# First expert's weights split ahead, and its first three chunks computed with the token rows stationary

## The reference

```python
x = x + hybrid_mixer(rms_norm(x, norm_mix), ...)      # ends in concatenate([...]) @ w_out
h = rms_norm(x, norm_ffn)
affinity = softmax(h @ w_router)                      # 16 experts
g, idx = top_k(affinity.T, cap)                       # cap: 128 rows of the sample, 64 of the prompt, per expert
xe = h[idx]
he = silu(xe @ w_gate) * (xe @ w_up)                  # 1024 -> 2048
ye = (he @ w_down) * g                                # 2048 -> 1024
x = x + zeros.at[idx].add(ye)                         # then a last rms_norm
```

## Time and profile before

| | us |
|---|---|
| median of 3 runs | 2579.83 (2577.54 to 2579.99) |
| profiled execution, its own time | 2577.25 |
| its span | 2575.5 |
| TensorE busy in the span | 2520.0 (98%) |
| VectorE busy | 1649.2 (64%) |
| ScalarE busy | 1366.9 (53%) |
| GpSimd busy | 266.7 (10%) |

### The profile page before, as it was taken

The page is one execution under the profiler, slowest core; times in us unless marked ns, Lnnn a source line. Parts: engine busy times, 40 slices in busy tenths (PEclk is TensorE's granted clock), DMA queues, the critical chain, the costliest instruction groups (busy, mean ns, idle before and its releaser), DMA issues.

```text
span 2575.5 us, 45337 instructions
## 1 busy us (share of the span) xinstructions
PE 2520.0 (98%) x18610; PEld 2278.5 (88%) x18610; DVE 1649.2 (64%) x1927; ACT 1366.9 (53%) x1559; POOL 266.7 (10%) x238
## 2 busy tenths in 40 slices
PE   8999999999987999999999999999999999999998
PEld 6777777787876999999999999999999999999997
DVE  6555555435387666767666676666767666676667
ACT  6434353424445555555556555555555556555556
POOL 3102020101101010010101101010010101101010
PEclk9999999999997999999999999999999999999999
DMA  4101010135327676676767667676676767667677
GB/s 158 31 17 55 2 55 2 61 122 209 138 96 298 229 253 234 247 252 228 252 228 252 240 241 252 228 252 233 247 252 228 252 228 252 240 241 252 228 253 282
DMA packets 62486, 503.73 MB, mean 196 GB/s; under 512 B 7568, under 2 KB 8080, under 8 KB 37808
## 3 DMA queue, kind: packets, MB, share of 16 engines
q1 hardware_dynamic: 46224, 448.88, 48.0%
q0 software_dynamic: 16160, 53.38, 7.0%
HBM read 465.07 MB, written 37.22 MB: 195 GB/s over the span
## 4 chain that ended last, share of the span: by engine, by line
PE 67%; DVE 1%; ACT 1%; DMA 0%; issue 0%; POOL 0%; POOLq 0%; DVEq 0%; ACTq 0%
PE up_banks_b L2025 15%; PE up_banks_a L2025 15%; PE up_banks_b L2028 6%; PE up_banks_a L2028 6%; PE up_banks_b L2061 2%; PE up_banks_b L2060 2%; PE up_banks_b L2059 2%; PE up_banks_b L2058 2%; PE up_banks_a L2062 2%; PE up_banks_b L2062 2%; PE up_banks_a L2059 2%; PE up_banks_a L2061 2%; PE up_banks_a L2058 2%; PE up_banks_a L2060 2%; PE up_banks_b L2023 1%; PE up_banks_a L2023 1%
## 5 line engine op out<-in xcount | busy, mean ns | idle before, releaser
L1842 DVE TENSOR_TENSOR big_lo<-ew_raw,big_hi 128x4096 fp32r<-128x4096 f32 x192 | 849.6, 4425 | 419.0 <-ACT big_hi L1653 418.9
L1653 ACT CAST big_hi<-ew_raw 128x4096 fp32r<-128x4096 f32 x192 | 697.3, 3632 | 506.5 <-PE up_banks_a L2025 223.7
L2025 PE MATMUL up_banks_b<-x_parts,big_hi 128*128 128x384 f32 x2048 | 582.9, 356 | 0.0
L2025 PE MATMUL up_banks_a<-x_parts,big_hi 128*128 128x384 f32 x2016 | 573.8, 356 | 0.0
L2028 PE MATMUL up_banks_b<-x_parts,big_lo 128*128 128x192 f32 x1792 | 449.0, 251 | 0.0
L2028 PE MATMUL up_banks_a<-x_parts,big_lo 128*128 128x192 f32 x1764 | 442.0, 251 | 0.0
L2025 PEld LDWEIGHTS up_banks_b<-x_parts,big_hi 128*128 128x128 f32 x2048 | 371.0, 189 | 0.0
L2025 PEld LDWEIGHTS up_banks_a<-x_parts,big_hi 128*128 128x128 f32 x2016 | 365.1, 189 | 0.6
L2028 PEld LDWEIGHTS up_banks_b<-x_parts,big_lo 128*128 128x128 f32 x1792 | 341.4, 191 | 0.0
L2028 PEld LDWEIGHTS up_banks_a<-x_parts,big_lo 128*128 128x128 f32 x1764 | 336.1, 191 | 0.6
L64 PE MATMUL bank<-big_hi,w_hi 128*128 128x512 f32 x576 | 236.8, 411 | 0.0
(11 more groups left out here) (320 smaller groups left out, 4076.3 us busy)
## 6 DMA issues: line engine op xcount, KB each, us to landing
ew_raw<-in_expert_weights SPq DMA_DIRECT2D x192, 2048.0 KB, 7.8
w_raw<-in_w_heads SPq DMA_DIRECT2D x48, 256.0 KB, 2.8
x_in<-in_x SPq DMA_DIRECT2D x12, 512.0 KB, 4.4
x_d<-in_x POOLq DMA_DIRECT2D x12, 512.0 KB, 4.1
residual<-x_d POOLq DMA_DIRECT2D x12, 512.0 KB, 2.9
ffn_in<-h_and_xT_d POOLq DMA_DIRECT2D x12, 512.0 KB, 2.9
ew_raw<-residual SPq DMA_DIRECT2D x12, 512.0 KB, 6.7
tab<-in_tables POOLq DMA_DIRECT2D x10, 512.0 KB, 7.6
```

Of the source, the lines that this page charges most:

```text
L1653: nc.scalar.copy(w_hi[:, c % RING], raw[:, c % RAW]).then_inc(hi_done, 1)
L1842: nc.vector.tensor_tensor(w_lo[:, c % RING], raw[:, c % RAW], w_hi[:, c % RING].bitcast(F32), ALU.subtract).then_inc(lo_done, 1)
L2025: last = nc.tensor.matmul(out[:, 0:2 * CAP], hi, x[:, k], start=n == 0, stop=n == KT - 1, skip_group_check=True)
```

## The change

A new class `ExpertStart` holds what both phases now share: the routing lists, the chunk buffers and the semaphores. Chunk c of an expert now lies in block (c + 1) mod 3 of `big_hi` and `big_lo`, so that chunks 0 and 1 take the places of the sample's tokens, whose products end first. The raw chunks 0 and 1 are loaded into the very bytes where their low parts will stand (`early_raw` is the memory of `big_lo`). What moves where:

- SyncE loads chunk 0 after tile 3's product, chunk 1 after tile 7's, chunk 2 after tile 11's; chunks 3 and 4 after the sample's and the prompt's rows are gathered.
- ScalarE casts chunk 0 at the start of its tiles 5 and 6, chunk 1 at 9 and 10, four casts of two row blocks each. VectorE subtracts the first half of chunk 0 in tile 6 and the second half in tile 7; chunk 1 whole, in the experts phase.
- The token list of the sample is turned at the end of the output phase, and GpSimd's queue gathers its rows there, ahead of the last store of h. The wait for all stores goes from the end of the phase to where the prompt's rows are asked for and to ScalarE's first cast of x.
- For chunks 0 to 2 of expert 0 the token rows are stationary and the weights move: per chunk 24 matmuls of 512 columns for the sample (`sample_high` 16, `sample_low` 8) and 16 for the prompt (`prompt_both`). The results stand by tokens; SiLU and product are made there, and 12 transposes (`turn_h`) bring them to the form that the down product needs. The body of expert 0 begins at chunk 3 and is written out on all engines.
- Rows are stored sample first; the last expert's store indices are swapped to match.

```diff
+class ExpertStart:
+    def place(self, big, c):
+        first = (c + 1) % self.RING * BLK
+        return big[:, :, first:first + BLK]
+    def load_early(self, sp, c):
+        sp.dma_start(self.place(self.early_raw, c), self.weights[0, c]).then_inc(self.raw_loaded[c], 16)
...
+        WEIGHTS_HIGH = {5: (0, slice(0, 4), False), 6: (0, slice(4, KT), True), 9: (1, slice(0, 4), False), 10: (1, slice(4, KT), True)}
+        WEIGHTS_LOW = {6: slice(0, 4), 7: slice(4, KT)}
...
+                for c in range(ahead.EARLY):
+                    sp.wait_ge(filled, 2 * CH * (c + 1))
+                    ahead.load_early(sp, c)
+                sp.wait_ge(filled, 2 * TT)
+                sp.dma_start(ahead.raw[:, 2], ahead.weights[0, 2]).then_inc(ahead.raw_loaded[2], 16)
...
+                        if t == TT:
+                            pool.wait_ge(h_stored, 16 * (TT - 1))
+                            pool.wait_ge(ahead.tokens_ready, 1)
+                            pool.indirect_dma_start(ahead.xs, None, h_dram[0:SEQS[1][1]],
+                                                    bass.IndirectOffsetOnAxis(token_of[:, 0, 0:1], 0))\
+                                .then_inc(ahead.gathered, 16)
...
                     dve.wait_ge(sum_inv, t + 1)
 
+                    if t in WEIGHTS_LOW and t == S_TILES - 1:
+                        ahead.low_early(dve, 0, WEIGHTS_LOW[t]).then_inc(ahead.lo_done, 1)
                     first, _, row = LISTS[list_of(t)]
                     nc.vector.tensor_scalar(affinity[:, t - first, row:row + NE], ex[:], stat[:, RSUM, t:t + 1], None, ALU.mult).then_inc(soft, 1)
...
+        X_SAMPLE_AFTER = 3
...
                 for slot in range(1, P_SLOTS):
                     take_best(choose, nc, table, table, best, where, 2, slot, P_SLOTS)
+                    if slot == X_SAMPLE_AFTER:
+                        first_x_low(0, S_HI, H_S_LO)
...
+                dve.wait_ge(first_rows_asked, 1)
+                sample_product(0)
+                ahead.low_early(dve, 1, slice(0, KT)).then_inc(lo_done, 1)
+                first_x_low(S_FIRST, P_HI, H_P_LO)
+                split(0, 2)
+                sample_product(1)
+                prompt_sum(0)
+                split(0, 3)
...
+                            if f == 0:
+                                pe.wait_ge(p_summed, 1)
+                            else:
+                                pe.wait_ge(h_lo_done, f)
...
+                pe.wait_ge(hi_done, ahead.EARLY)
                 pe.wait_ge(turned_lo, S_FIRST)
+                sample_high(0)
+                sample_low(0)
+                sample_high(1)
+                pe.wait_ge(chosen, 2)
+                for i, lists in enumerate((chosen_gate, chosen_token)):
+                    nc.tensor.transpose(s_bank[0][:, i * ROWS:(i + 1) * ROWS], lists, ident[0:ROWS, 0:ROWS]).then_inc(back, 1)
+                pe.wait_ge(hi_done, BY_TOKENS)
+                sample_high(2)
                 pe.wait_ge(gathered, 32)
                 for r in range(KT // 2):
                     turn_prompt(r, r).then_inc(turned, 1)
+                pe.wait_ge(lo_done, 2 + RAW)
+                sample_low(1)
+                pe.wait_ge(tokens_ready, 7)
+                pe.wait_ge(turned_lo, 2 * S_FIRST)
+                prompt_both(0)
+                prompt_both(1)
+                pe.wait_ge(lo_done, BY_TOKENS + RAW)
+                sample_low(2)
+                prompt_both(2)
```

More of the change, by code:

```diff
@@ L1159, in _ @@
                     head_high(LATE_HEADS.get(t, ()))
+                    if t in WEIGHTS_HIGH:
+                        c, tiles, last = WEIGHTS_HIGH[t]
+                        for k in range(tiles.start, tiles.stop, 2):
+                            made = ahead.high_early(act, c, slice(k, k + 2))
+                        if last:
+                            made.then_inc(ahead.hi_done, 1)
                     act.wait_ge(added, 2 * t + 2)
@@ L1255, in sample_rounds @@
                             merge_lists(then, nc, best, where, 0, CAP_S, merged, spare)
+                            dve.sem_inc(ahead.chosen, 1)
                 for t in range(TT):
@@ L1277, in _ @@
                         prompt_sums((2, 3))
+                    if t in WEIGHTS_LOW and t < S_TILES - 1:
+                        ahead.low_early(dve, 0, WEIGHTS_LOW[t])
+                    if t == TT - 1:
+                        dve.wait_ge(ahead.back, 1)
+                        nc.vector.tensor_copy(token_of[:, 0:NE, 0], banks[0][:, 0:NE]).then_inc(ahead.tokens_ready, 1)
                     sample_rounds(PAUSES[t][1])
@@ L1439, in _, with experts_phase @@
                     route(t)
+                pe.wait_ge(ahead.chosen, 1)
+                pe.wait_ge(added, 2 * (TT - 2) + 1)
+                nc.tensor.transpose(banks[0][:, 0:NE], chosen_rows, ident[0:NE, 0:NE]).then_inc(ahead.back, 1)
                 turn_affinities(len(LISTS) - 1)
-def experts_phase(nc, weights, identity, norm_final, h_dram, acc, outs, routing, big_hi, big_lo):
+def experts_phase(nc, weights, norm_final, h_dram, acc, stored, outs, ahead):
     with ExitStack() as ctx:
@@ L1493, in experts_phase @@
         const_loaded = sem("const_loaded_f")
[L1494 to L1496 removed]
+        raw_loaded, hi_done, lo_done = ahead.raw_loaded, ahead.hi_done, ahead.lo_done
         chunk_done = sem("chunk_done")
@@ L1644, in body @@
                     pool.sem_inc(rows_free, 1)
-                experts(pool, body)
+                experts(pool, body, first=0)
             @block.scalar
@@ L1732, in end_squares, with first_x_high @@
                     end_prompt_square(i)
-                split(0, 0)
-                for first, cols in ((0, S_HI), (S_FIRST, P_HI)):
+                act.sem_inc(lowered, 2 * BY_TOKENS)
+                act.sem_inc(silu_ready, BY_TOKENS)
+                def first_x_high(first, cols):
                     for r in range(KT // 2):
@@ L1917, in h_low @@
                         last.then_inc(h_lo_done, 1)
-                    for c in range(CHUNKS):
+                    for c in range(first_chunk, CHUNKS):
                         if c == UPS:
@@ L2008, in up_chunk, with sample_high, sample_low @@
-                def up_chunk(e, c):
+                def sample_high(c):
+                    for k in range(KT):
+                        nc.tensor.matmul(sample_bank[c], x[:, k, S_HI], ahead.hi(c)[:, k], start=k == 0, stop=False)
+                        nc.tensor.matmul(sample_bank[c], x[:, k, H_S_LO], ahead.hi(c)[:, k], start=False, stop=False)
+                def sample_low(c):
+                    for k in range(KT):
+                        last = nc.tensor.matmul(sample_bank[c], x[:, k, S_HI], ahead.lo(c)[:, k], start=False, stop=k == KT - 1)
+                    last.then_inc(sample_made, 1)
@@ new lines, in prompt_both, with turn_h @@
+                def prompt_both(c):
+                    for k in range(KT):
+                        nc.tensor.matmul(prompt_bank[c], x[:, k, H_P_BOTH], ahead.hi(c)[:, k], start=k == 0, stop=False)
+                        last = nc.tensor.matmul(prompt_bank[c], x[:, k, H_P_BOTH], ahead.lo(c)[:, k], start=False, stop=k == KT - 1)
+                    last.then_inc(chunk_done, 1)
+                def turn_h(c):
+                    pe.wait_ge(h_made, max(NTH_SAMPLE[c], NTH_PROMPT[c]))
+                    for i in range(2):
+                        part = slice(i * P, (i + 1) * P)
+                        nc.tensor.transpose(h_bank[c][:, i, S_HI], sample_h[c][:, part], ident[:])
+                        last = nc.tensor.transpose(h_bank[c][:, i, P_HI], prompt_h[c][:, part], ident[0:CAP_P, 0:CAP_P])
+                    last.then_inc(h_turned, 1)
@@ L2031, in up_chunk @@
                             last.then_inc(gates_done, 1)
-                    last.then_inc(chunk_done, 1)
+                        if first and c == BY_TOKENS and f >= 1:
+                            if f == 3:
+                                last.then_inc(chunk_done, 1)
+                            turn_h(f - 1)
+                    if not (first and c == BY_TOKENS):
+                        last.then_inc(chunk_done, 1)
                 def last_down_chunk(e, c, i, part):
@@ L2065, in _ @@
                 pe.sem_inc(chunk_done, RING)
-                pe.wait_ge(const_loaded, 16)
-                def keep_running(count):
-                    for _ in range(count):
-                        nc.tensor.transpose(set_b[:, 3, 0:P], ident[:], ident[:])
-                for rows, wait in ((NE, 0), (ROWS, 1)):
-                    if wait:
-                        pe.wait_ge(choosing, ROUND_STEPS)
-                        keep_running(8)
-                        pe.wait_ge(chosen, wait)
-                    for i, lists in enumerate((chosen_gate, chosen_token)):
-                        nc.tensor.transpose(s_bank[0][:, i * ROWS:i * ROWS + rows], lists[0:rows, 0:CAP_S], ident[0:rows, 0:rows])\
-                            .then_inc(back, 1)
```

(1 more changed line is left out.)

338 lines of the change are left out of this document (208 added, 130 removed).

## The result

The changed kernel takes 2604.44 us (median of 4 runs, 2601.58 to 2606.47) against 2579.91 (4 runs) for the kernel before: ratio 1.0096, 95% interval 1.0078 to 1.0113. It is 24.5 us slower. The forecast was 2578.8, with a range up to 2583.6. The profiled execution has a span of 2604.0 us, 28.5 more than that of before (2575.5); it is one of the slower of its kernel and that of before one of the faster of its own.

What follows compares the result with a forecast made beforehand. TensorE, busy 98% of the span, was taken to bound the kernel. Chunk 5 sooner (-5.0), tile 7 and list copy (+2.4) and one clock fall (+1.6) gave -1.0 on 2579.83: 2578.8 us, range 2573.0 to 2583.6.

Steps and rivals of the forecast that it cites:

- From there both kernels are the same on TensorE, and the lead stays: From chunk 5 of expert 0 on: TensorE's work is unchanged, so the 5.0 us lead is kept.
- Tile 7, +2.4: VectorE's half-chunk subtraction ahead of `affinity` makes TensorE 2.2 us later; the last tile's token list copy adds 0.2.
- First product 11.5 sooner: Start of expert 0: the sample's rows are gathered earlier, so the first product starts at 786.2 instead of 797.74.
- Low clock at the start, 1.8 lost: First product of expert 0: after idling, TensorE runs 3.7 us at the lower clock, losing 1.8 us.
- Waits of 1.3 and 1.9 at the prompt's rows: Expert 0: TensorE waits 1.3 us for the prompt's gathered rows, then 1.9 for chunk 1's low part.
- Form at no cost: Chunks 0 to 2 of expert 0: 40 matmuls of 512 columns take 9.10 us a chunk, the old form 9.12.
- Chunks 3 and 4: Expert 0: chunk 3 takes 9.12 us plus 1.2 of transposes; chunk 4's last block waits 3.0 for h's low parts.
- Chunk 5 sooner by 5.0, less 1.6 for a fall: Expert 0: chunk 5 starts at 841.5 instead of 846.5; one clock fall, at 802, costs 1.6 us.
- the first: Rival: the waits in chunk 4 (3.0 us) and tile 7 (2.2) are absent, total -7.8; chance 0.24.
- The prompt's late gather: Rival at expert 0's prompt rows: landing takes 10.5 us, total +5.4, 2585.2 us; chance 0.12 together with the next rival.
- about 9.1 us a chunk from chunk 5 on: Sign that the forecast is right: TensorE's pace from chunk 5 of expert 0 on.

Runs made afterwards that it cites:

- e12: Changed kernel with 480 unused bytes behind `next_token`: 2577.17 us, ratio 1.0004 to the kernel before.
- e4: Kernel before with 32 unused bytes ahead of and 32 behind `x_parts`, which also moved `h_parts` by 64 bytes: 2600.90 us, ratio 1.0090.
- e14: Kernel before with 64 unused bytes ahead of `big_hi`, so all buffers move and their distances stay: 2579.14 us, ratio 1.0008.
- e11: Changed kernel with 224 unused bytes behind `next_token`: 2578.94 us, ratio 1.0008 to the kernel before.
- e13: e12 with chunk 0's low part all in tile 6, list transposes before chunk 1's sample matmuls, h's low parts before the chunk's: 2570.01 us, ratio 0.9974.
- e6: e5 with the low part of chunk 0 made in tile 6 alone, none in tile 7: 2603.64 us.
- e1: Changed kernel with 32 unused bytes behind `next_token`: 2597.62 us, ratio 1.0074 to the kernel before.
- e5: Changed kernel with 96 unused bytes behind `next_token`, so later buffers begin on a multiple of 128 bytes: 2606.03 us, ratio 1.0108 to the kernel before.
- e7: e6 with the two transposes of the chosen lists ahead of the 16 sample matmuls of chunk 1 on TensorE: 2599.59 us.
- e9: Kernel before with 8 unused columns per tile of `x_parts` and `h_parts`, each tile 32 bytes further on: 2595.72 us, a single run.

## Why the prediction was wrong, point by point

**The step that failed** is "From there both kernels are the same on TensorE, and the lead stays". The instructions are the same; the places of their operands are not, and I gave the move of every buffer behind `next_token` no line in the sum. It cost 1.53 us an expert. By the ratios the move cost 24 us (24.5 us of loss with it, 0.3 in e12 without it). The difference of two profiled executions is larger, and tells where it lies. By stages, from the profile after less that of e12, which differ in nothing but the 480 bytes: 21.4 us between the first and the last scatter, 1.3 behind it, 1.7 from the last tile to the first scatter, 0.5 from tile 7 to the last tile, and 3.6 in tiles 0 to 7, of which 1.7 is a fall of the clock near 610. The profile after shows that fall:

```profile
606.00:616.00 10.00, 7.53 (x27) 5.63 (x26) 8.22 (x12) 4.96 (x9) 1.05 (x2) 0.83 0.73 256
```

The change is not needed for it: e4 and e14, whose instructions are those of the kernel before, have a clock of 0.91 over 600 to 620 too, and e11 and e13, at a distance of 0, as well. Ahead of 610 there are another 2.8, of which 1.5 in the transform behind 570 and 1.3 ahead of it, where the two run the same instructions at the same addresses and only the executions differ. That is 31.3 in all, 3.0 of which (the fall and the 1.3) are differences of executions. The profile after exceeds that of before by 2.8 less, since e12's span is 2.8 under that of before.

**The rest of the sum** can be judged in e12, where this term is away. Its timeline of TensorE:

```profile
721.80 0.62 PE L1467 MATMUL bank_d<-ident_e,affinity 128*48 128x128 f32 x4 [2.65 <-DVE affinity L1367]
771.44 1.97 PE L1477 MATMUL bank_d<-ident_e,x_d 128*128 128x128 f32 x8 [3.01 <-DVE x_d L1334]
788.05 0.76 PE L2157 MATMUL up_banks_a<-big_hi,x_parts 128*128 128x512 f32 x1 [3.01 <-DVE x_parts L2018]
841.28 0.44 PE L2204 MATMUL up_banks_a<-x_parts,big_hi 128*128 128x384 f32 x1 [0.95 <-DVE h_parts L1998]
```

- Tile 7, +2.4: right. The wait is 2.65 (0.45 + 2.2), and from the start of this wait to the last tile it takes 2.2 more than before. e6 took the wait away, and its median is 2.4 lower. The clock fell behind this wait in e1, e5 and e11 (0.50 to 0.55 in the stretch 724 to 726) and not in e12 and the profile after: the sum had no fall there, and one execution does not tell it.
- First product 11.5 sooner: 16.61 us after the last tile's rows are taken up instead of 27.82, 11.2.
- Low clock at the start, 1.8 lost: right in e12, where the first product starts at 788.05 and the granted clock is 0.50 up to 790 and 0.57 over 790 to 792, so 1.8 lost. That is one execution: in e6 it is 0.50 to 794 and 0.73 over 794 to 796 with the first product at 788.91, so 3.1 lost. The row that the term was taken from holds 0.2 us more than the 3.2 read from it: 0.90 at both ends and 3 us between them are 3.4.
- Waits of 1.3 and 1.9 at the prompt's rows: 0.75 and 1.89 in the profile after. There the gather is asked for at 807.73 and ends TensorE's wait at 811.15, 3.4 later and not 3.8. e7 shows that the order of TensorE's queue makes them, as the text said. (The text has gathers and weight loads share DMA queues; on the profile page before they stand in queues of their own, q0 and q1, and share only the 16 engines.)
- Form at no cost: right at a distance of 0. The last 16 token matmuls of chunk 2 take 3.63 us in e12, 0.227 each, and 3.73 in the profile after. The Trainium skill's formula for single matmuls (TensorE: Matmul & The Clock Gate, Back-to-back issue gap), which made the old form cheaper, finds no support here either.
- Chunks 3 and 4: the parts were wrong, the sum right. In chunk 3 the transposes of h cost 2.8 us (it takes 11.94 in e12, less 9.12), not 1.2, and the wait in chunk 4 is 0.95, not 3.0; chunk 4 takes 10.49, 1.4 over 9.12. A TensorE that comes 1.6 later to chunk 4 finds as much less of the wait. That it was still shorter by some 0.4, and that 2.8 + 1.4 make the forecast's 1.2 + 3.0, is luck. From the start of chunk 3 to that of chunk 5 it is 22.4, as forecast.
- Chunk 5 sooner by 5.0, less 1.6 for a fall: 4.3 sooner in e12, counted from the last tile. No clock fell at the new waits in it, nor in the profile after:

```profile
806.00:808.00 2.00, 2.00 (x10) 1.53 (x10) 0.92 (x6) 0.00 (x0) 0.45 (x2) 1.00 0.02 4
811.00:816.00 5.00, 2.97 (x14) 2.32 (x15) 5.00 (x6) 0.91 (x5) 3.57 (x4) 1.00 0.80 269
```

It did in e1 and e6, behind waits of the same size, and not in e5, e11 and e12. So one execution does not tell it; the forecast should have given that fall a chance and not a place in the sum.

For what the change is about the forecast was -1.0 us, no change that can be told. e11 and e12 measured 2.0 and 0.3 over the kernel before beside them, ratios whose intervals hold 1: the same verdict, from parts some of which were wrong. Of the rivals, the first had the waits in tile 7 and chunk 4 absent, -7.8. As the change is written they are there, that in chunk 4 at a third of its size. e13 takes both away and the two at the prompt's rows too, and gives -6.9; that the two numbers are near is chance, since they are not made of the same waits. The prompt's late gather did not come. No rival had the pace of a matmul in it, and "about 9.1 us a chunk from chunk 5 on" was the sign that failed: 9.17 and more.

## What to carry to other kernels

Before a new small buffer is put ahead of large ones, look where TensorE's two operands come to lie against each other, and pad so that their distance modulo 256 bytes stays what it was: here 32 bytes cost some 25 us, and 224 or 480 unused bytes behind them gave them back. When a change makes TensorE busier without more instructions, compare the mean of one matmul of the same line and shape before looking for waits. And in a queue, put what starts a long chain (here two transposes of lists) ahead of work that no one waits for.

## What the runs showed of the hardware

In these runs the pace of fp32 matmuls whose stationary operand changes each time depends on the distance in a partition between stationary and moving operand. With a multiple of 256 bytes a 512-column matmul starts every 226.7 ns; in the kernel before each step from the eleventh of a half on, but for the last, is within 0.2 of it (means over 12 experts). Timeline of TensorE in the kernel before, some in a row:

```profile
1325.77 0.39 PE L2059 MATMUL up_banks_a<-big_hi,h_parts 128*128 128x512 f32 x1
1325.99 0.39 PE L2060 MATMUL up_banks_a<-big_lo,h_parts 128*128 128x512 f32 x1
1326.22 0.39 PE L2061 MATMUL up_banks_a<-big_hi,h_parts 128*128 128x512 f32 x1
1326.44 0.39 PE L2062 MATMUL up_banks_a<-big_lo,h_parts 128*128 128x512 f32 x1
```

At distances of 32, 64 and 128 the steps go up and down between 226 and 242 ns (the same means, the first step of a half aside), 233.2 on average. For the up chunks, whose matmuls have 384 and 192 columns, the loss is smaller: 0.07, 0.02 and 0.11 us over the 64 of a chunk at 32, 64 and 128, against 0.26 over the 40 of a down chunk. The Trainium skill (SBUF — State Buffer, Operand start alignment) speaks of the operand's address for legality only, and says that those runs timed nothing; its section "A bandwidth-pool intuition that's wrong" gives weight loads a read port of their own. These runs agree that the load itself does not get longer, 188 ns in both, yet the matmul beside it does. What in the chip does this is not shown. Two reads that meet in one part of the memory would fit e14, and e9's tiles, which lie well and are slow among neighbours that do not, would fit a rhythm that has to settle over several matmuls; neither was tested by itself. Distances other than 0, 32, 64 and 128 modulo 256 were not tried alone.
